# The second input projection of a two-block transformer in seven block products, with gates and x staged in memory

## The reference

```python
x = first_block(x, c, ...)          # short convolution layer, stick-breaking attention layer, then
                                    # rmsnorm(x, final_norm_g): this x is the residual of the second block
h = _rmsnorm(x, norm1_g[l]) * (1.0 + scale1) + shift1
proj = h @ w_in[l]                  # 4352 columns
qa, ka, va, qd, kd, vd, ga, gd = jnp.split(proj, points, axis=-1)
out_a = _sliding_window_attention(qa, ka, va, swa_sinks[l], slopes_swa)
out_d = _diff_attention(qd, kd, vd, lam, lam_init, diff_subln_g[l], slopes_diff)
merged = sigmoid(ga) * (out_a @ w_branch_swa[l]) + sigmoid(gd) * (out_d @ w_branch_diff[l])
x = x + gate1 * (merged @ w_out[l])
h2 = _rmsnorm(x, norm2_g[l]) * (1.0 + scale2) + shift2
u = h2 @ w_up; a, g = split(u, 2); a = causal 3-tap convolution of a, + conv_b
x = x + gate2 * ((gelu(a) * g) @ w_down)
return _rmsnorm(x, final_g)
```

## Time and profile before

| | |
|---|---|
| median of 3 runs | 2812.82 us (2809.76 to 2816.41) |
| the profiled execution | 2811.65 us, its span 2809.8 us |
| TensorE busy | 2636.7 us (94% of the span) |
| VectorE, ScalarE, GpSimd busy | 1399.4 us (50%), 1004.0 us (36%), 900.2 us (32%) |
| share of TensorE in the chain that ended last | 80% |
| second input projection, 30 units after the quad | 1349.3 to 1680.3 us |

### The profile page before, as it was taken

The page is one execution under the profiler, slowest core; times in us unless marked ns, Lnnn a source line. Parts: engine busy times, 40 slices in busy tenths (PEclk is TensorE's granted clock), DMA queues, the critical chain, the costliest instruction groups (busy, mean ns, idle before and its releaser), DMA issues.

```text
span 2809.8 us, 34152 instructions
## 1 busy us (share of the span) xinstructions
PE 2636.7 (94%) x12543; PEld 2194.4 (78%) x12543; DVE 1399.4 (50%) x1890; ACT 1004.0 (36%) x1697; POOL 900.2 (32%) x642
## 2 busy tenths in 40 slices
PE   3899999999899999999999998878996999999998
PEld 2688888788788899987888878767875888887887
DVE  5766665640324566657400007764567777772112
ACT  3400012521410688846111017661254555551000
POOL 1133331022233566610332330233105332225664
PEclk7999999999999999999999999999998999999999
DMA  5244453353365544432443127213241333338833
GB/s 214 87 138 137 137 151 108 98 176 112 128 209 165 132 113 111 99 122 74 151 142 141 46 60 178 78 39 105 75 150 49 116 105 120 105 105 291 297 91 122
DMA packets 362931, 356.95 MB, mean 127 GB/s; under 512 B 35299, under 2 KB 283532, under 8 KB 362508
## 3 DMA queue, kind: packets, MB, share of 16 engines
q1 hardware_dynamic: 341036, 294.47, 35.7%
q10 hardware_dynamic: 21728, 60.30, 5.6%
HBM read 277.64 MB, written 77.07 MB: 126 GB/s over the span
## 4 chain that ended last, share of the span: by engine, by line
PE 80%; DVE 10%; ACT 4%; DMA 3%; POOL 2%; issue 1%; SPq 0%; DVEq 0%; ACTq 0%; POOLq 0%
PE PS L1582 40%; PE PS L1667 13%; PE PS L1708 8%; PE PS L694 5%; PE PS L1626 3%; PE PS L672 2%; PE PS L1649 2%; DMA mod_raw<-in_w_ada 1%; PE PS L658 1%; PE PS L657 1%; PE PS L1753 1%; DVE prob L1048 1%; POOL opBf L1555 1%; DVE M L2281 1%; PE PS L817 1%
## 5 line engine op out<-in xcount | busy, mean ns | idle before, releaser
L1582 PE MATMUL PS<-opA,w_hi 128*128 128x512 f32 x3264 | 1021.9, 393 | 18.8 <-POOL w_lo L1391 13.7
L1582 PEld LDWEIGHTS PS<-opA,w_hi 128*128 128x128 f32 x3264 | 618.1, 189 | 151.4 <-POOL w_lo L1391 16.1
L1582 PE MATMUL PS<-opA,w_lo 128*128 128x512 f32 x1632 | 639.6, 392 | 0.0
L1386 POOL CAST w_hi<-w_raw 128x1024 fp32r<-128x1024 f32 (+1 forms) x150 | 155.6, 1037 | 1117.4 <-PE PS L1582 708.7
L1391 POOL TENSOR_TENSOR w_lo<-w_raw,w_hi 128x1024 fp32r<-128x1024 f32 (+1 forms) x152 | 368.2, 2422 | 89.5 <-ACT w_hi L1953 77.5
L1582 PEld LDWEIGHTS PS<-opA,w_lo 128*128 128x128 f32 x1632 | 309.3, 190 | 63.8 <-issue 0.2
L2281 DVE SCALAR_TENSOR_TENSOR M<-mod_raw,small,M 128x512 f32<-128x512 f32 x168 | 169.6, 1010 | 169.7 <-DMA mod_raw<-in_w_ada 87.9
L2563 DVE SCALAR_TENSOR_TENSOR X<-PS,mod,X 128x512 f32<-128x512 f32 x64 | 48.0, 751 | 297.4 <-PE PS L1708 206.3
L1667 PE MATMUL PS<-opB,Xr 128*128 128x512 f32 x640 | 176.2, 393 | 5.7 <-ACT M L2167 5.7
L1667 PE MATMUL PS<-opA,Xr 128*128 128x512 f32 x560 | 160.9, 398 | 8.7 <-DVE M L2693 5.8
L1582 PE MATMUL PS<-opB,w_hi 128*128 128x512 f32 x512 | 159.9, 391 | 2.8 <-DVE opB L2551 1.4
(11 more groups left out here) (236 smaller groups left out, 4368.1 us busy)
## 6 DMA issues: line engine op xcount, KB each, us to landing
mod_raw<-in_w_ada SPq DMA_DIRECT2D x96, 256.0 KB, 3.0
z_dram<-opB ACTq DMA_DIRECT2D x44, 512.0 KB, 3.9
w_raw<-in_w_in SPq DMA_DIRECT2D x34, 512.0 KB, 3.8
w_raw<-in_a_w_in SPq DMA_DIRECT2D x32, 512.0 KB, 4.8
q_dram<-stage ACTq DMA_DIRECT2D x16, 1024.0 KB, 4.0
hin<-q_dram SPq DMA_DIRECT2D x64, 256.0 KB, 5.9
w_raw<-in_w_down SPq DMA_DIRECT2D x32, 512.0 KB, 4.5
opA<-z_dram SPq DMA_DIRECT2D x60, 256.0 KB, 5.4
```

Source lines behind the costliest of these rows:

```text
L1386: pool.tensor_copy(hi, raw).then_inc(pool_done, 1)
L1582: ins = pe.matmul(ps, w[:, k0 + k, :], rhs(part, k0 + k), start=(k == 0 and n == 0), stop=(k == chunks - 1 and n == 2))
```

## The change

- Of the 34 units of the second input projection the quad stays; the other 30 become 15 pairs of seven block products, with the functions of the feed-forward (`sevens`, `weight_sums`, `weight_high`, `weight_low`, `snap`, `block_sum`), which now take the stage `q` as an argument.
- The result of a pair is no more read out of PSUM by one copy: VectorE's block sums put it into a tile, ScalarE writes its high part or, through the sigmoid, the gate, VectorE the low part, into one staging place per column block (`in2_stage`), and ScalarE's queue stores it. Each use of the place waits until the store before it has landed.
- The gates go to memory (`gate_dram`) and come back during the attention (16 transfers on SP); so does the norm factor (`rstd_dram`).
- x is written out unscaled, in two halves, and scaled after the attention, between the merges of the branches.
- Sums of token blocks are made by VectorE instead of GpSimd, in both stages, between the low parts of weights; ScalarE's and VectorE's lists at the opening of the feed-forward are reordered (`snap(q, 0, 2)` ahead of gelu and first tap; low parts of the P6 sums ahead of those of P5).
- Loads for the attention wait for products of the last pair instead of the last unit.

```diff
+SEVENS = {U_IN2: 15, U_FFN: FC - 2}
...
             for row in range(2):
+                sp.wait_ge(in2_stored[row], at("in2_stored", in2_unit(LAST_IN2, row)))
+            for n in range(2 * KC):
+                sp.dma_start(gates[:, n, :], gate_dram[n]).then_inc(gates_in, 16)
...
-            sp.wait_ge(x_out, at("x_out", 1))
+            sp.wait_ge(pe_done, at("seven", U_IN2, LAST_IN2, P7))
+            sp.wait_ge(dve_done, at("seven_w", U_IN2, LAST_IN2, P3))
             swa_keys_values(0)
-            sp.wait_ge(pe_done, at("unit", U_BRANCH - 1, 1))
+            sp.wait_ge(pe_done, at("seven", U_IN2, LAST_IN2, P3))
             for c in range(4):
                 queries(c)
...
                 if u == U_BRANCH + 3:
-                    reload(1)
+                    reload_rstd()
+                    for j in range(KC):
+                        reload_half_spilled(U_IN2, j)
...
-            for n in range(4, 34):
-                unit(U_IN2 + n, opA, turned=U_IN2 + n - 1 if 13 < n <= 18 else None)
+            for i in range(SEVENS[U_IN2]):
+                sevens(U_IN2, i)
...
+            def in2_use(i, row):
+                u, tile = in2_unit(i, row), block_tile(U_IN2, i, row)
+                kind = in2_kind(u)
+                if i >= 0 and kind != "value":
+                    act.wait_ge(dve_done, at("block", U_IN2, i, row, 0))
+                    act.wait_ge(dve_done, at("block", U_IN2, i, row, 1))
+                if i > -2:
+                    act.wait_ge(in2_stored[row], at("in2_stored", in2_unit(i - 1, row)))
...
+                for i in range(1, SEVENS[q]):          # ScalarE's list of one pair
+                    turned = [in2_kind(in2_unit(i - 1, row)) == "value" for row in range(2)]
+                    snap(q, i, 0)
+                    weight_high(q, i + 1, P1)
+                    weight_high(q, i, P3)
+                    if not turned[0]:
+                        in2_use(i - 1, 0)
+                    weight_high(q, i + 1, P2)
+                    if not turned[1]:
+                        in2_use(i - 1, 1)
+                    snap(q, i, 1)
+                    weight_high(q, i + 1, P6)
+                    weight_high(q, i + 1, P5)
...
+                    in2_store(i - 1, 0)
+                    snap(q, i, 2)
+                    in2_store(i - 1, 1)
+                    weight_high(q, i + 1, P7)
+                    weight_high(q, i + 1, P4)
...
-            for n, i in enumerate(QUAD_ORDER + tuple(range(4, 13))):
-                hl_lo(U_IN2 + i, small[:, QS + n:QS + n + 1] if n < 4 else -QSCALE if n < 8 else 1.0)
-                if n < KC:
-                    scale_x("fin1", "final_norm_g", n, 0)
-                    scale_x("fin1", "final_norm_g", n, 1)
+            in2_dve()
             second_dve(dve)
+            dve.wait_ge(gates_in, at("gates_in"))
```

More of the change, by code:

```diff
@@ L95, with in2_unit, in2_kind, in2_place @@
 QUAD_ORDER = (2, 3, 0, 1)
+def in2_unit(i, row):
+    return U_IN2 + {-2: 2, -1: 0}.get(i, 4 + 2 * i) + row
+def in2_kind(u):
+    return "parts" if u < U_IN2 + 13 else "value" if u < U_IN2 + 18 else "gate"
+def in2_place(u):
+    n = u - U_IN2
+    return QUAD_ORDER.index(n) if n < 4 else n
 def down_unit(hf, g, n):
@@ L1682, in sevens, with values_out @@
-                products(P6, False, False)
-                pe.wait_ge(dve_done, at("fu", f - 2, 0, 1) if i >= 2 else at("fz", i, 0))
-                products(P5, True, False)
-                pe.wait_ge(act_done, at("snap", f, 1))
+                    step(pe_done, "seven", q, i, which)
+                def values_out(row):
+                    u = in2_unit(i - 2, row)
+                    if q == U_IN2 and i >= 2 and in2_kind(u) == "value":
+                        pe.wait_ge(act_done, at("in2_used", u))
@@ new lines, in sevens @@
+                products(P6, False, False)
+                if i < 2 and q == U_FFN:
+                    pe.wait_ge(dve_done, at("fz", i, 1))
+                elif i < 2:
+                    pe.wait_ge(act_done, at("in2_copy", in2_unit(i - 2, 1)))
+                else:
+                    pe.wait_ge(dve_done, at("block", q, i - 2, 0, 1))
+                    pe.wait_ge(dve_done, at("block", q, i - 2, 1, 0))
+                values_out(1)
+                products(P5, True, False)
+                if q == U_IN2:
+                    for row in range(2):
+                        if i and in2_kind(in2_unit(i - 1, row)) == "value":
+                            turn_block(i - 1, row)
@@ L2740, in _ @@
             other_taps(2, 0)
-            for i in range(SEVENS):
+            for i in range(SEVENS[q]):
                 f = i + 2
```

686 lines of the change are left out of this document (449 added, 237 removed).

## The result

The changed kernel takes **2780.14 us** (median of 4 runs, 2779.05 to 2787.82) against 2812.54 (2809.76 to 2816.41) of the kernel before: ratio **0.989**, 95% interval 0.9874 to 0.9906. Measured once more beside later kernels it was 2781.02 (2780.71 to 2782.77), ratio 0.989, 0.9873 to 0.9907. The change is worth about 1.1%. The forecast was 2780.

The account below looks back on a forecast made before the run. TensorE, busy for 94% of the span, was taken as the bound. From 2811.65 us: -25.8 (37.9 gained less 12.1 lost), +2 at the attention's entry, -8.0 in the feed-forward gave 2779.9, stated as 2780; 8-in-10 range 2765 to 2795.

Parts of the forecast that it names:

- Pairs: Second input projection: 15 pairs at 19.23 us replace 30 units at 10.88 us, a gross gain of 37.9 us.
- Its opening: First two pairs of the second input projection: waits and slow products lose 12.1 us against two pairs at pace.
- What GpSimd takes: Both openings: each GpSimd weight sum running beside VectorE's sums costs VectorE 0.9 us.
- Locked out: Rival, both openings: VectorE stands still for each whole weight sum, 1.7 us, total 2790; chance 0.17 together with late keys.
- Attention's entry: Start of the attention: TensorE waits longer for queries, whose loads are issued later; 2 us lost, bounds 0 and 5.
- Gates and x: Attention and branches: loading gates back and scaling x later cost 0; late keys, some 5 us, if loads were slower.
- The feed-forward's opening: First two pairs of the feed-forward: no wait at P1, 10.6 us at second pair's P6; gain 8.0, bounds 0 and 17.
- The rival "slower": Second input projection: store landings over 13 us make snap 1 late in 13 pairs, gain gone at 15.5 us; chance 0.04.
- that cover: Second input projection's stores: some 10 us to land before their place is wanted, cost nothing unless landing takes over 13 us.

Follow-up runs that it names:

- experiment 6: Changed kernel with GpSimd's four weight sums of the second pair held until VectorE's last low part for P1 and P2, at both openings: 2780.40 us, ratio 0.9895.
- experiment 5: Changed kernel with the first key-value head's values loaded behind the first queries instead of ahead of them: 2777.11 us, ratio 0.9873.
- experiment 1: Changed kernel with the feed-forward's opening as before the change, token sums on GpSimd and old list orders: 2795.26 us, ratio 0.9932.
- Experiments 3 and 4: Changed kernel with one, then two of ScalarE's copies out of PSUM moved earlier in the feed-forward's second pair: 2781.30 us, then 2783.69 us.
- experiment 7: Changed kernel with each store of queries and keys in the second input projection issued twice, 2796.57 us, or three times, 2831.14 us.

## Why the prediction was right

**Pairs.** Right, 2.9 us too small: 19.23 us a pair was taken from the feed-forward, whose pairs vary from 19.04 to 19.4, and the new stage holds the bare 84 x 0.2267 = 19.04 wherever no transposes fall in. TensorE has no wait at all in it from the third pair on. VectorE is busy for 108 of 252 us there and for 265 of 350 in the feed-forward; that this is the reason was not tested.

**Its opening.** 12.1 forecast, 12.3 measured. The third pair starts at 1399.6 against 1399.9, P1 at 1354.8 against 1356.3 (the norm's end came 1.7 earlier than the row that I started from). From the norm to P1's low part it is 23.8 us against the 24.7 of the forecast, to P2's 24.6; and the last thing that P1 waited for was ScalarE's copy of a unit of the quad, 0.4 us behind P2's low part, which the forecast had put behind P1. P3's wait was 2.0 instead of 0.9, since four stores hold ScalarE for 3.9 us and not for 2.4, and the second pair's was 0.7 instead of 2.3. These wander: the repeat has 1.2 and 2.3. That the sum fits to 0.2 us is luck in part: the forecast had 10.2 us of waits and one slow product, measured were 8.3 us of waits and 4.0 that are mostly slow products.

**What GpSimd takes.** 0.9 us a sum was forecast and 0.96 measured by moving four of them away (experiment 6). *Locked out* has fallen as a price: nothing like 1.7 us a sum was won back. As a mechanism it is what the rows show. An operation of VectorE that meets a running sum ends 0.55 us behind it, so it stands still until that sum is nearly over, and a sum that meets a running operation of VectorE takes 1.53 us instead of 1.29. The price is 0.96 and not 1.7 because the 1.7 us from one sum to the next hold one operation of VectorE, 0.72 us of its work, which is not lost. So the sentence of the forecast that the row of 1.66 us is "about half of what a full lock would take" was wrong: 1.66 is what the lock gives, and the sum was right because it used the row and not the rule. The Trainium skill (SBUF — State Buffer, Who interferes with whom) calls the shared port "an exclusive lock", and counts VectorE's operations with two inputs in SBUF among those that contend. The trace agrees, with VectorE's end 0.55 us behind GpSimd's; what the forecast had wrong was the price that it put on the lock. And the two engines meet here without a semaphore, other than the opening section says.

**Attention's entry.** 2 taken, 3.8 measured in the first profile and up to 4.7 in the others, inside the bounds. The step named the right cause (values ahead of the queries) and priced it low; experiment 5 takes back all of it.

**Gates and x.** Nothing, as forecast: no wait for keys at the second differential head, 0.4 us in the branches.

**The feed-forward's opening.** 8.0 forecast, 7.9 measured, undone by experiment 1. P1 does not wait, the first pair ends 25.9 us behind the quad (26.5 forecast), and the wait that I put at P6 of the second pair (10.6) is there (11.3). The forecast gave two causes in one breath, the snap's place behind six other items and the inputs of these, which hang on VectorE's list. Experiments 3 and 4 show that the place alone is worth nothing; that the rest is work which VectorE has not done yet is read from the rows, and not tested by a run.

**The rival "slower".** It did not come, and the mechanism that it named was wrong. Landing never came near 13 us, so that cover was not put to the test. What failed is the count of 0.6 us for each issue: what slows the kernel with more stores is ScalarE held at their issue ahead of a snap. The gain of the change is used up between two and three times the stores.

## What to carry to other kernels

A wait of the busy engine for an item in another's list can be a debt of work and not a matter of order: before you move the item, look whether that engine, or the one that it waits for, has gaps (operations of 0.69 us every 0.80 have none). When work goes from GpSimd to VectorE, count what the one takes from the other while both run, and read single operations for it, not merged rows; here a sum of GpSimd that meets VectorE's costs it 0.96 us, more than the 0.72 that doing it itself would take. A total that fits can hide two errors: compare the terms. And a store can hold the engine that issues it, here for 1.3 us instead of 0.6 from the fourth of a group on: put it behind the copy that is waited for only if nothing behind it is waited for next.

## What the runs showed of the hardware

- VectorE's sum of two 128x512 tiles in SBUF and GpSimd's take turns, one whole operation each, every 1.70 us. VectorE's ends 0.55 us behind GpSimd's, GpSimd's 1.15 behind VectorE's. Alone VectorE makes one every 0.72 us; GpSimd's takes 1.29 us if it comes first and 1.53 in turn. With one input in PSUM VectorE's keeps its 0.69 us.
- Stores of 0.5 MB on ScalarE's queue: 0.6 us to issue the first two, 0.9 the third, 1.3 each behind them, while the copies still land in 5.2 us (experiment 7). Twelve, in two groups of six, hold the engine for 14 us.
- Two transfers of 256 KB ahead of the queries delay them by 3.8 us, in other profiles by up to 4.7 (experiment 5).
- Behind a gap TensorE's granted clock was 0.78 in the mean over 24 matmuls and 0.61 over 12, which took 7.18 and 4.60 us instead of 5.6 and 3.0.
- The stretch up to the quad's end, whose instructions are the same in twelve profiles, took from 1347.4 to 1358.6 us. The executions of one kernel vary too (2773.3 to 2785.7). What chooses between them is open.
